# Rows scaled before they are transposed, half-slot waits split, and the router's gain moved into the rows

## The chip, the cores and the metric

The kernel runs on one core of a Trainium2 chip. The metric is device microseconds of one execution, lower is better; the time of a kernel is the median of its runs. The engines are TensorE (PE, its weight loads PEld), VectorE (DVE), ScalarE (ACT), GpSimd (POOL) and SyncE (SP), which here only issues the transfers of weights.

## The reference

Two blocks run on one sequence of 256 rows of width 1024, all in fp32. The first has two layers: attention and a gated convolution with a SwiGLU MLP (width 2816), then a spatial gating layer with a mixture of experts (eight SwiGLU experts of width 2816, two per row), each layer closed by a gated per-layer embedding. The second has two layers of four kinds of attention side by side and a squared-ReLU MLP of width 4096, modulated by columns that a vector `c` gives. Every part starts with an RMS norm:

```python
def rms_norm(x, g):
    xf = x.astype(jnp.float32)
    y = xf * lax.rsqrt(jnp.mean(xf * xf, axis=-1, keepdims=True) + RMS_EPS)
    return (y * g.astype(jnp.float32)).astype(x.dtype)
```

What matters here: x times one number per row, then times one number per column (in the second block also a column sum is added), then a product with weights.

## The kernel before, in words

**Weights.** They come as a stream of slots of 128x2048 fp32 (1 MB) into a ring of six in SBUF. SP waits until a slot has been split and refills it (L485 to L489). To multiply in fp32 precision, each half slot (128x1024) is split in two: ScalarE copies it rounded to fp32r as `w_hi` (L2001), VectorE subtracts to get `w_lo` (L1242). There are three pairs of such half buffers, four with the experts. A product is three matmuls, hi x hi, hi x lo and lo x hi (`product`, L515 to L519). `half_slot` (L510) makes TensorE wait until a half's `w_lo` is ready; ScalarE may write the next `w_hi` into a pair once the half in it is done. So a half buffer turns round in the order TensorE, ScalarE, VectorE, TensorE.

**Order.** Every engine's program is written out by hand, in one order; nothing is planned at run time. `split_to(m)` on ScalarE and VectorE puts the splits up to half m at that place of the program, and `reach(n)` says how far they can go when n halves are done.

**Norms.** There are eleven, numbered k = 0 to 10: 0 to 5 in the first block (4 is the router's), 6 to 9 in the second, 10 at the end. The rows lie in `resid`, 128 partitions x two row blocks t x 1024. `add_branch` (L1360) adds a layer's result, t = 0 first; ScalarE sums squares (`square_rows`), VectorE asks for the root (`ask_root`), POOL takes it (L2399). `scale` (L1299) then makes, for each t, a diagonal matrix `diag` of the 128 roots (L1310). `norm` calls it for t = 1 between two weight splits. On TensorE, `rowsT` (L529) multiplies each 128x128 block of the rows by `diag`, so that the block comes out in PSUM transposed and scaled in one (L537): four blocks of t = 0, then after a second wait four of t = 1, four of t = 0, four of t = 1. Ahead of it stand 18 dummy matmuls (`keep_warm`, L526) for k = 1, 6, 7, 9. From PSUM, ScalarE makes `x_hi` with the column gain (L2056), VectorE `x_lo` (L1351); in the second block both first modulate into `xT` (L1335 and L2048), then split (L2064 and L1349). For the router (k = 4) alone the rows themselves are scaled (L1303), transposed by the identity (L535) and multiplied by the gain into `xT` (L1329).

**The ends of a layer.** `row_product` goes through the halves of an output matrix; for a layer's output its last three go through `last_rows` (L601), and so do the last two of each MLP and of each embedding. It takes all its halves for row block 0 and then all for row block 1, so that block 0 is done early. It waits for all of its halves ahead of the first product (L603).

**Experts.** After the router, `select` (L1728) makes for each expert a 0/1 matrix `sel` from row to place in a chunk of 128, and `selg`, the same times the gate. TensorE's `gather` (L868) multiplies the scaled rows by `sel` into PSUM banks 6 and 7. `take` (L1738) on VectorE multiplies them by the norm's gain into `xT` (L1742), ScalarE's `take` (L2207) copies to `x_hi` (L2211), VectorE subtracts to `x_lo` (L1748). An expert has eleven steps j (`moe_step` on each engine): TensorE multiplies four halves up, transposes the previous step's hidden rows (L893), and multiplies two halves down. In step 6 of an expert VectorE selects for the next expert, in step 7 TensorE gathers, in step 8 both `take`. In step 1 VectorE splits the previous expert's result (`split_y`, L1764) behind the weight splits and ahead of the hidden rows' split (`moe_lo`, L1751); steps 2 and 3 scatter and merge. `selg` is read only by the second pass, a branch that runs when an expert has over 128 rows; these inputs don't take it.

## Time and profile before

| | |
|---|---|
| median of 3 runs | 2150.4 us (2150.29 to 2153.49) |
| the profiled execution | 2146.43 us, span 2144.7 us |
| granted TensorE clock, mean over the span | 0.966 |
| busy: PE, DVE, ACT, POOL | 1989.4, 1595.2, 1192.9, 27.9 us |

A line of a group gives the line of the kernel, the engine and operation, what is written from what, the count, and after the bar the busy time and the mean duration. In a timeline a line is one instruction or a run of equal ones: start, length, engine, line, operation, count, and in square brackets the idle time of the engine ahead of it and what ended it. A matmul's length is longer than the distance to the next, because they are pipelined; distances are read from starts. PEclk is the share of full speed (2.4 GHz) that was granted, 0.50 is 1.2 GHz.

### The profile page before, as it was taken

How to read it: one execution, taken by the hardware profiler on the slowest of the kernel's cores; microseconds unless marked ns; L12 is line 12 of the kernel's file. 1: busy time of each engine (PE TensorE's matmuls, PEld its weight loads, DVE VectorE, ACT ScalarE, POOL GpSimd, SP SyncE). 2: the span in 40 equal slices, each digit the busy share in tenths (PEclk: the TensorE clock that was granted, in tenths of full speed). 3: DMA queues.
4: the chain of work that ended last, by engine and by line, in shares of the span. 5: the costliest groups of instructions: out<-in, count | busy, mean ns of one | idle time of the engine just before them, and what ended most of it. 6: DMA issues, size and time to landing. Idle time of an engine off the chain costs nothing.

```text
span 2144.7 us, 28118 instructions
## 1 busy us (share of the span) xinstructions
PE 1989.4 (93%) x11190; PEld 1714.1 (80%) x11190; DVE 1595.2 (74%) x2014; ACT 1192.9 (56%) x1638; POOL 27.9 (1%) x32
## 2 busy tenths in 40 slices
PE   7879999976999999999999999898899999989998
PEld 7859998865878787878787777688789988868997
DVE  4657887455988989898989899568568984746555
ACT  4334334433877777777777778456444445634443
POOL 0000000000000000000000000000000000000000
PEclk9989999898999999999999999899999999989999
DMA  7416886432988888888888899433148973214551
GB/s 284 157 59 237 345 334 242 167 116 90 365 330 341 326 335 334 326 340 333 333 338 332 330 342 349 184 119 117 41 168 337 351 283 137 101 38 148 190 183 60
DMA packets 71263, 511.52 MB, mean 239 GB/s; under 512 B 8146, under 2 KB 8530, under 8 KB 9682
## 3 DMA queue, kind: packets, MB, share of 16 engines
q1 hardware_dynamic: 69536, 504.40, 62.4%
q10 hardware_dynamic: 1588, 5.24, 0.7%
q8 instruction: 91, 1.49, 0.3%
q14 instruction: 48, 0.39, 0.0%
HBM read 508.56 MB, written 1.05 MB: 238 GB/s over the span
## 4 chain that ended last, share of the span: by engine, by line
PE 79%; DVE 13%; ACT 5%; issue 2%; POOL 1%; DMA 0%; ACTq 0%; POOLq 0%; SPq 0%; DVEq 0%
PE ps L517 23%; PE ps L519 23%; PE ps L518 22%; DVE w_lo L1242 6%; ACT w_hi L2001 3%; PE ps L537 2%; PE ps L875 1%; PE ps L722 1%; PE ps L526 1%; PE ps L674 1%; PE ps L688 1%; PE ps L893 1%; PE ps L780 1%; ACT score L2109 1%; DVE arena L1228 1%
## 5 line engine op out<-in xcount | busy, mean ns | idle before, releaser
L1242 DVE TENSOR_TENSOR w_lo<-ring,w_hi 128x1024 fp32r<-128x1024 f32 x862 | 1043.2, 1222 | 373.3 <-ACT w_hi L2001 347.4
L2001 ACT ACTIVATE w_hi<-ring 128x1024 fp32r<-128x1024 f32 x862 | 909.9, 1060 | 704.9 <-PE ps L519 697.8
L517 PE MATMUL ps<-w_hi,x_hi 128*128 128x512 f32 (+1 forms) x1072 | 416.9, 391 | 29.1 <-DVE w_lo L1242 20.1
L519 PE MATMUL ps<-w_hi,x_lo 128*128 128x512 f32 (+1 forms) x1072 | 408.4, 383 | 0.0
L518 PE MATMUL ps<-w_lo,x_hi 128*128 128x512 f32 (+1 forms) x1072 | 407.9, 383 | 0.0
L517 PE MATMUL ps<-x_hi,w_hi 128*128 128x256 f32 x1248 | 357.9, 287 | 4.4 <-DVE x_lo L1351 3.8
L518 PE MATMUL ps<-x_lo,w_hi 128*128 128x256 f32 x1248 | 354.5, 284 | 0.0
L519 PE MATMUL ps<-x_hi,w_lo 128*128 128x256 f32 x1248 | 354.4, 284 | 0.0
L517 PE MATMUL ps<-w_hi,h_hi 128*128 128x512 f32 (+1 forms) x716 | 286.0, 399 | 23.0 <-DVE h_lo L1755 18.6
L518 PE MATMUL ps<-w_lo,h_hi 128*128 128x512 f32 (+1 forms) x716 | 279.4, 390 | 0.0
L519 PE MATMUL ps<-w_hi,h_lo 128*128 128x512 f32 (+1 forms) x716 | 279.2, 390 | 0.0
L517 PEld LDWEIGHTS ps<-w_hi,x_hi 128*128 128x128 f32 (+1 forms) x1072 | 197.4, 184 | 72.2 <-DVE w_lo L1242 24.3
L517 PEld LDWEIGHTS ps<-x_hi,w_hi 128*128 128x128 f32 x1248 | 241.0, 193 | 8.3 <-DVE w_lo L1242 4.0
L518 PEld LDWEIGHTS ps<-x_lo,w_hi 128*128 128x128 f32 x1248 | 240.9, 193 | 1.7 <-issue 0.2
L519 PEld LDWEIGHTS ps<-x_hi,w_lo 128*128 128x128 f32 x1248 | 240.6, 193 | 0.0
L519 PEld LDWEIGHTS ps<-w_hi,x_lo 128*128 128x128 f32 (+1 forms) x1072 | 197.2, 184 | 41.5
L518 PEld LDWEIGHTS ps<-w_lo,x_hi 128*128 128x128 f32 (+1 forms) x1072 | 197.7, 184 | 37.9
L517 PEld LDWEIGHTS ps<-w_hi,h_hi 128*128 128x128 f32 x716 | 134.7, 188 | 68.1 <-DVE h_lo L1755 37.2
L519 PEld LDWEIGHTS ps<-w_hi,h_lo 128*128 128x128 f32 x716 | 134.7, 188 | 29.0
L518 PEld LDWEIGHTS ps<-w_lo,h_hi 128*128 128x128 f32 x716 | 135.0, 189 | 24.4
L1228 DVE SCALAR_TENSOR_TENSOR arena<-ring,csilu,arena 128x1024 f32<-128x1024 f32 x88 | 108.9, 1278 | 0.0
L2109 ACT ACTIVATE score<-score,soft 128x128 f32<-128x128 f32 (+4 forms) x112 | 47.2, 423 | 35.5 <-DVE soft L1421 35.5
(266 smaller groups left out, 1490.6 us busy)
## 6 DMA issues: line engine op xcount, KB each, us to landing
ring<-in_stream SPq DMA_DIRECT2D x479, 1024.0 KB, 4.9
con<-in_consts ACTq DMA_DIRECT2D x1, 2048.0 KB, 21.6
resid<-in_x SPq DMA_DIRECT2D x1, 1024.0 KB, 6.3
arena<-in_ln_rows ACTq DMA_DIRECT2D x2, 512.0 KB, 4.5
arena<-in_fin_row ACTq DMA_DIRECT2D x2, 512.0 KB, 3.5
out<-rows SPq DMA_DIRECT2D x2, 512.0 KB, 2.6
arena<-in_w_s ACTq DMA_DIRECT2D x1, 512.0 KB, 5.7
con<-in_consts ACTq DMA_DIRECT2D x1, 237.0 KB, 4.1
```

Of the source, the lines that this page charges most:

```text
L517: pe.matmul(out_, lhs[0], rhs[0], start=start, stop=False)
L518: pe.matmul(out_, lhs[0], rhs[1], start=False, stop=False)
L519: return pe.matmul(out_, lhs[1], rhs[0], start=False, stop=stop)
L526: pe.matmul(ps[:, b, :], x_hi[:, 6, 0:P], x_lo[:, 4:6, :].rearrange("p a s -> p (a s)"), start=True, stop=True)
L537: return pe.matmul(at, src[:, t, c], diag[:, t, :], start=True, stop=True)
L674: last = pe.matmul(ps[:, b + u // 2, (u % 2) * S:(u % 2) * S + kw], q, k, start=True, stop=True)
L688: last = pe.transpose(ps[0:kp, 4 + n // 4, (n % 4) * P:(n % 4 + 1) * P], score[:, g % 2, u, kb * P:kb * P + kp], ident)
L722: last = pe.matmul(ps[:, mix_bank(layer, g), o * vw:(o + 1) * vw], probT[0:kp, g % 2, u * nkb + kb, :], v, start=kb == 0, stop=kb == nkb - 1)
L1228: ins = dve.scalar_tensor_tensor(out=acc[:, part, :], in0=src, scalar=c, in1=acc[:, part, :], op0=ALU.mult, op1=ALU.add)
L1242: dve.tensor_tensor(lo, ring[:, q % RING, a:a + HALF], hi.bitcast(F32), ALU.subtract)\
L2001: act.activation(half_buffer(m)[0], ring[:, q % RING, a:a + HALF], ACT.Copy).then_inc(hi_ready, 1)
L2109: ins = act.activation(sc, sc, ACT.Exp, bias=soft[:, g % 4, 0, u:u + 1], scale=96.0 ** -0.5 if kind == "mla" else 0.125, accum_out=soft[:, ...
```

## The change

It has four parts. `scale` writes scaled rows of 1024 in place of the diagonal, t = 0 in one operation and t = 1 in two halves (from `resid` to `rows`, in norm 6 from `rows` to `resid`), and `rowsT` transposes them by the identity in all norms, with a third wait before the last four blocks. `last_rows` waits for each half just ahead of its first product. The router's gain is read as a row spread over all partitions, into a buffer that the spatial layer's bias had; it goes into the rows with the scaling, so that what was a multiply after the transpose is a copy, and `take` reads PSUM directly on both engines. `selg` is left out of the first pass, and in step 1 `split_y` goes ahead of the last of four weight splits.

```diff
@@ build: names
+        moe_gain = ln_b
-        diag = ff[:, 2, 0:2 * P].rearrange("p (t s) -> p t s", t=QB)
@@ rowsT
                 def turn(t, f):
                     at = ps[:, 4 + f // 2, (f % 2) * S + t * P:(f % 2) * S + (t + 1) * P]
                     c = slice(f * P, (f + 1) * P)
-                    if k == 4:
-                        return pe.transpose(at, rows[:, t, c], ident)
-                    src = rows if k == 6 else resid
-                    return pe.matmul(at, src[:, t, c], diag[:, t, :], start=True, stop=True)
-
-                def scaled(t):
-                    if k == 4:
-                        pe.wait_ge(rows_scaled, t + 1)
-                    else:
-                        pe.wait_ge(diag_ready, 2 * NORM_AT[k] + t + 1)
+                    return pe.transpose(at, (resid if k == 6 else rows)[:, t, c], ident)
+
+                def scaled(n):
+                    pe.wait_ge(rows_scaled, 3 * k + n)
 
                 if k in (1, 6, 7, 9):
                     keep_warm(18, 2)
-                scaled(0)
+                scaled(1)
                 for f in range(4):
                     turn(0, f)
-                scaled(1)
+                scaled(2)
                 for f in range(KT):
                     if f == 4:
                         for late in range(4, KT):
                             turn(0, late)
+                        scaled(3)
                     last = turn(1, f)
@@ last_rows
-                w = [half_slot(m + n, 1) for n in range(len(lhs))]
+                w = []
                 for t in range(QB):
                     for n in range(len(lhs)):
+                        if t == 0:
+                            w.append(half_slot(m + n, 1))
                         row_part(w[n], t, lhs[n], b0, start and n == 0, n == len(lhs) - 1)
@@ VectorE: scale
-                if k == 4:
-                    dve.tensor_scalar(rows[:, t, :], resid[:, t, :], stat[:, t:t + 1], None, ALU.mult)\
-                        .then_inc(rows_scaled, 1)
-                elif k == 10:
+                if k == 10:
...
                 else:
                     r = stat[:, 2 * t + 1:2 * t + 2] if k == 6 else stat[:, t:t + 1]
-                    dve.tensor_scalar(diag[:, t, :], ident, r, None, ALU.mult).then_inc(diag_ready, 1)
+                    src, dst = (rows, resid) if k == 6 else (resid, rows)
+                    if k == 4:
+                        dve.wait_ge(moe_gain_in, 16)
+                        for c in (slice(0, BANK), slice(BANK, D)):
+                            ins = dve.scalar_tensor_tensor(out=rows[:, t, c], in0=resid[:, t, c], scalar=r,
+                                                           in1=moe_gain[:, c], op0=ALU.mult, op1=ALU.mult)
+                            if (t, c.start) != (0, 0):
+                                ins.then_inc(rows_scaled, 1)
+                        return
+                    for c in [slice(0, D)] if t == 0 else [slice(0, BANK), slice(BANK, D)]:
+                        dve.tensor_scalar(dst[:, t, c], src[:, t, c], r, None, ALU.mult).then_inc(rows_scaled, 1)
@@ VectorE: norm, k == 4
-                        src = ps[:, 4 + b, :].rearrange("p (f s) -> p f s", f=2)
-                        dve.tensor_tensor(xT[:, 2 * b:2 * b + 2, :], src, bc(gain[:, 2 * b:2 * b + 2], S), ALU.mult)\
+                        dve.tensor_copy(xT[:, 2 * b:2 * b + 2, :].rearrange("p f s -> p (f s)"), ps[:, 4 + b, :])\
                             .then_inc(gained, 1)
@@ VectorE: select
-                    dve.tensor_scalar(sel[:, t, :], rank, pl, None, ALU.is_equal)
-                    ins = dve.tensor_scalar(selg[:, t, :], rank, pl, gate[:, t, e], ALU.is_equal, ALU.mult)
+                    ins = dve.tensor_scalar(sel[:, t, :], rank, pl, None, ALU.is_equal)
+                    if w is second_pass:
+                        ins = dve.tensor_scalar(selg[:, t, :], rank, pl, gate[:, t, e], ALU.is_equal, ALU.mult)
@@ VectorE: take
-                for h in range(2):
-                    dve.wait_ge(w.gather_ready, counts[h])
-                    dve.tensor_tensor(xT[:, 4 * h:4 * h + 4, 0:P],
-                                      ps[:, 6 + h, :].rearrange("p (f c) -> p f c", f=4),
-                                      bc(gain(4)[:, 4 * h:4 * h + 4], P), ALU.mult).then_inc(w.gathered, 1)
                 for h in range(2):
                     dve.wait_ge(w.gathered_hi, counts[h])
                     f = slice(4 * h, 4 * h + 4)
-                    dve.tensor_tensor(x_lo[:, f, c0:c0 + P], xT[:, f, 0:P], x_hi[:, f, c0:c0 + P].bitcast(F32),
+                    dve.tensor_tensor(x_lo[:, f, c0:c0 + P], ps[:, 6 + h, :].rearrange("p (f c) -> p f c", f=4), x_hi[:, f, c0:c0 + P].bitcast(F32),
                                       ALU.subtract).then_inc(w.gathered_lo, 1)
@@ VectorE: moe_step
                 if s >= 1:
+                    if j == 1 and e >= 1:
+                        split_to(reach(2 * n + 1))
+                        split_y(e - 1)
                     split_to(reach(2 * (n + 1)))
-                    if j == 1 and e >= 1:
-                        split_y(e - 1)
                     moe_lo(s - 1)
@@ ScalarE: after the four Gelus of the spatial layer
+            act.wait_ge(vn_ready, 2)
+            act.dma_start(moe_gain, ln_rows[2].partition_broadcast(P)).then_inc(moe_gain_in, 16)
             keep_cat(4, 2)
@@ ScalarE: take
-                    act.wait_ge(w.gathered, counts[h])
+                    act.wait_ge(w.gather_ready, counts[h])
                     f = slice(4 * h, 4 * h + 4)
-                    act.activation(x_hi[:, f, c0:c0 + P], xT[:, f, 0:P], ACT.Copy).then_inc(w.gathered_hi, 1)
+                    act.activation(x_hi[:, f, c0:c0 + P], ps[:, 6 + h, :].rearrange("p (f c) -> p f c", f=4), ACT.Copy)\
+                        .then_inc(w.gathered_hi, 1)
```

The host packs the router's gain `lf[1]` as a third row of `ln_rows`.

## Rows read from the trace of the kernel before

**Rows 1.** The page, part 1: busy time of each engine.
```profile
PE 1989.4 (93%) x11190; PEld 1714.1 (80%) x11190; DVE 1595.2 (74%) x2014; ACT 1192.9 (56%) x1638; POOL 27.9 (1%) x32
```

**Rows 2.** Stretches: length, busy PE, PEld, DVE, ACT, POOL, PEclk, DMA share, GB/s.
```profile
500.00:527.00 27.00, 15.38 (x90) 14.36 (x90) 11.92 (x49) 4.15 (x10) 0.55 (x1) 0.68 0.00 0
...
527.00:1356.00 829.00, 798.17 (x3648) 644.59 (x3648) 739.68 (x792) 618.09 (x740) 0.00 (x0) 1.00 0.89 335
...
502.60:506.00 3.40, 2.73 (x12) 2.33 (x12) 2.34 (x4) 0.00 (x0) 0.00 (x0) 0.50 0.00 0
506.00:509.40 3.40, 3.11 (x28) 3.12 (x28) 0.23 (x1) 0.00 (x0) 0.00 (x0) 1.00 0.00 0
```

**Rows 3.** The waits of PE: releaser, us in total, times, longest.
```profile
PE ps L537 <- DVE ff L1310: 25.9, 9, 9.8
...
PE ps L517 <- DVE h_lo L1755: 18.6, 22, 1.3
```

**Rows 4.** Timeline of PE in `last_rows` ahead of norm 9.
```profile
1933.30 0.39 PE L519 MATMUL ps<-w_hi,x_lo 128*128 128x512 f32 x1
1936.25 0.76 PE L517 MATMUL ps<-w_hi,x_hi 128*128 128x512 f32 x1 [2.56 <-DVE w_lo L1242]
...
1937.23 0.63 PE L519 MATMUL ps<-w_hi,x_lo 128*128 128x512 f32 x1
```

**Rows 5.** The same in three other places.
```profile
151.85 0.47 PE L517 MATMUL ps<-w_hi,x_hi 128*128 128x512 f32 x1 [2.56 <-DVE w_lo L1242]
...
1560.89 0.76 PE L517 MATMUL ps<-w_hi,x_hi 128*128 128x512 f32 x1 [2.56 <-DVE w_lo L1242]
...
349.99 0.47 PE L517 MATMUL ps<-w_hi,h_hi 128*128 128x512 f32 x1 [0.67 <-DVE w_lo L1242]
```

**Rows 6.** Timeline of DVE, the first expert, behind the gather and in step 8.
```profile
594.58 1.23 DVE L1242 TENSOR_TENSOR w_lo<-ring,w_hi 128x1024 fp32r<-128x1024 f32 x1 [3.42 <-ACT w_hi L2001]
...
605.87 1.28 DVE L1742 TENSOR_TENSOR xT<-ps,con 128x512 f32<-128x512 f32 x2
607.25 1.29 DVE L1748 TENSOR_TENSOR x_lo<-xT,x_hi 128x512 fp32r<-128x512 f32 x2
608.80 4.63 DVE L1242 TENSOR_TENSOR w_lo<-ring,w_hi 128x1024 fp32r<-128x1024 f32 x4 [0.26 <-ACT w_hi L2001]
```

**Rows 7.** Timeline of ACT in the same step 8.
```profile
604.27 0.37 ACT L2235 ACTIVATE arena<-ps 128x256 f32<-128x256 f32 x1
606.59 1.23 ACT L2211 ACTIVATE x_hi<-xT 128x512 fp32r<-128x512 f32 x2 [1.95 <-DVE xT L1742]
```

**Rows 8.** Timeline of PE in the same step and the next.
```profile
608.60 0.38 PE L893 MATMUL ps<-con,arena 128*128 128x128 f32 x2
610.08 0.50 PE L517 MATMUL ps<-w_hi,x_hi 128*128 128x512 f32 x1 [1.10 <-DVE w_lo L1242]
...
613.82 0.50 PE L517 MATMUL ps<-w_hi,h_hi 128*128 128x512 f32 x1 [0.70 <-DVE h_lo L1755]
```

**Rows 9.** Timeline of PE: twelve blocks behind the second wait, norms 4, 7, 8.
```profile
502.54 2.79 PE L535 MATMUL ps<-con,rows 128*128 128x128 f32 x12 [1.64 <-DVE rows L1303]
...
1576.40 2.95 PE L537 MATMUL ps<-ff,resid 128*128 128x128 f32 x24 [0.58 <-DVE ff L1310]
...
1767.05 5.46 PE L537 MATMUL ps<-ff,resid 128*128 128x128 f32 x24 [1.78 <-DVE ff L1310]
```

**Rows 10.** DVE's lines by source: durations in ns (least, median, most), first and last start.
```profile
L1310 DVE TENSOR_SCALAR ff<-con,stat x18: 277/284/289, 9.4 to 1951.4; 128x128 f32<-128x128 f32 x18
...
L1303 DVE TENSOR_SCALAR rows<-resid,stat x2: 746/750/753, 499.4 to 501.7; 128x1024 f32<-128x1024 f32 x2
...
L1735 DVE TENSOR_SCALAR arena<-con,place,gate x16: 337/341/345, 518.8 to 1207.7; 128x128 f32<-128x128 f32 x16
```

**Rows 11.** Timeline of DVE in norm 7, behind the weight split.
```profile
1577.39 0.99 DVE L1335 TENSOR_SCALAR xT<-ps,modg,ada 128x256 f32<-128x256 f32 x2
```

More of the change, by code:

```diff
@@ L340, in build @@
         ln_in = sem("ln_in")
+        moe_gain_in = sem("moe_gain_in")
         fin_in = sem("fin_in")
@@ L412, in __init__ @@
                 self.gather_ready = sem(name + "gather_ready")
-                self.gathered = sem(name + "gathered")
                 self.gathered_hi = sem(name + "gathered_hi")
@@ L2606, in lay_out @@
         "lam": np.ascontiguousarray(np.asarray(i["a_lambda"])[0].reshape(-1)),
-        "ln_rows": np.stack([np.asarray(i["c_ln_g"])[0], np.asarray(i["c_ln_b"])[0]]),
+        "ln_rows": np.stack([np.asarray(i["c_ln_g"])[0], np.asarray(i["c_ln_b"])[0], lf[1]]),
         "w_s": np.ascontiguousarray(np.asarray(i["c_w_s"])[0].transpose(2, 0, 1)),
```

1 line of the change is left out of this document (removed).

## The prediction, made before the changed kernel was run

> **What bounds the kernel now.** The page's busy line comes first [rows 1]: TensorE works in 93% of the span, VectorE in 74%. So the time is TensorE's work, its clock, and the holes in it; a microsecond is won where TensorE waits or works less. The stage table shows where the holes are small in share but many: the experts' 829 us have TensorE busy for 798.2 of them, at full clock, with VectorE busy for 739.7 [rows 2]. The waits of TensorE name the releasers: 25.9 us in nine waits for the diagonal (one for each norm but the router's), and 18.6 us for `h_lo` L1755, nearly all with the experts [rows 3]. The timeline then shows single places: the last halves of a branch [rows 4, 5], the gather for the next expert [rows 6 to 8], the transposes of the rows [rows 9] and VectorE's part of them [rows 10, 11].
>
> **Part 1: waits one by one in last_rows.** Now the call waits for all its halves, then multiplies. In the branch before the last norm the previous product would have been followed at 1933.53 (start 1933.30 plus a pitch of 0.23), but the next starts at 1936.25, when the third half's `w_lo` is in [rows 4]. Halves one and two were split before, or that wait would name them in turn. Each is six matmuls in the first row block, 6 x 0.227 = 1.36 us, so with single waits TensorE reaches the third half at 1933.53 + 2.72 = 1936.25, just as it is ready. The hole closes: 2.72 us, and 0.08 for the slower first pitch behind a hole. Here and at 1560.89 the granted clock also fell to 1.2 GHz behind the hole (two matmuls from 1936.25 to 1937.23 take 0.98, against 0.46 at 2.4 GHz [rows 4]); eight such matmuls at 0.43 for 0.23, an estimate, are 1.6 us more. In the other two branches the matmul behind the hole has its full-clock length, 0.47 against 0.76 us [rows 5], and nothing more is won. Four branches: 2 x 2.8 + 2 x 4.35 = 14.3. Two calls with two halves (the first MLP's end, at 349.99, and one like it) wait 0.67 for the second half [rows 5]: about 0.9 each, 1.8. The third such call and the two of the gated embedding show no hole: 0. What is behind the waits on TensorE's queue is the same; ScalarE and VectorE wait for the second row block as before, and all move up. Sum **-16.1**; bounds 13 (the clock falls anyway, and 0.4 us stays at each third half) and 18.
>
> **Part 2: the gain leaves the gather.** In step 8 of seven experts VectorE multiplies two halves (1.28 us), ScalarE, idle for 1.95, copies them, and VectorE subtracts (1.29); its split of weights starts at 608.80 only [rows 6, 7]. TensorE has done its pair of transposes at 608.60 and should go on some 0.14 later (an estimate, as no hole-free pair is among the rows), but goes on at 610.08, and at 613.82, after 12 matmuls and another hole, where it would without one be at about 612.95 [rows 8]. The loss is 1.34 + 0.86 + 2 x 0.07 = 2.34 us. After: ScalarE copies from PSUM right behind the activation at 604.27, so 604.64 to 605.87; the subtraction can start where the multiply did, 605.87, and ends at 607.16. Four splits, 4.63, end at about 611.75 (their `w_hi` come in time, since ScalarE is 1.85 earlier), and `h_lo` at 612.05 to 612.15. TensorE wants it at 608.74 + 12 matmuls = 611.5: a loss of 0.6 to 0.7 stays. Won: 1.66 x 7 = **-11.6**. From below 0.8 each (a source in PSUM slows ScalarE, or the backlog is paid in the next step), from above 2.3: 5.6 to 16. The `selg` operations (341 ns, two per expert [rows 10]) go away in step 6; the gather hides them, as VectorE idles for 3.42 us behind it [rows 6]: 0. The exchange of split_y with the fourth split changes no total before `h_lo`, as three splits still come first: 0, bounds 0.7 either way in seven places. Ahead of the first expert nothing hides this chain: one 0.34 that no longer delays the gather plus its neighbour's issue, and one multiply: **-1.2**.
>
> **Part 3: the router's norm.** Two products of whole rows (750 ns [rows 10]) become two pairs of halves with the gain row, about 0.7 each by the 0.64 to 0.69 of a 512-wide operation with two inputs [rows 6]. The first pair's excess lies beside ScalarE's squares; in the second TensorE starts on the first half, at the same time. The four gain multiplies become copies of as many elements. Taken 0, bounds -0.4 and +0.5. The added transfer (ScalarE's queue, 0.5 MB spread over partitions) waits for VectorE's last use of that buffer; ScalarE's next work then is the concatenation, for which it waits anyway: 0. It lands tens of microseconds ahead of its use. SP's and POOL's queues get nothing new; POOL only sees its roots asked for 0.47 later in two norms where VectorE's whole-row product is directly ahead (the first and the sixth); the sixth pays it, and it is in the sum below.
>
> **Part 4: transposes for the diagonal, nine norms.** A 128x128 product with the diagonal is two matmul records, a transpose one: x24 is twelve blocks [rows 9]. At full clock twelve take 2.95 us, at 1.2 GHz 5.46; twelve transposes took 2.79 at 1.2 GHz, so half. TensorE saves 1.5 or 2.7 us behind the second wait. Against it VectorE: 283 ns become 0.75 us for row block 0 and two halves of some 0.48 for block 1 (between 283 and 750 ns by elements), of which the first delays the transposes by 0.2 and both delay the weight split behind them by 0.6. How it comes out depends on what follows:
> - Plain norms at full clock (the second and third): TensorE ended after the first `x_lo`, so it gains, until VectorE paces it: -0.3 and -0.5.
> - Modulated norms at full clock (before each MLP): the modulation starts at 1577.39 with no idle time ahead of it, right behind the weight split [rows 11]. VectorE is the bound, the 0.6 is lost: +0.6 each, +1.2.
> - Five norms at 1.2 GHz (first, fourth, sixth, and the first of each block): 2.7 less 0.2 to 0.6, and less what the products now do at the low clock, as they begin before it rises (the 5.46 us of [rows 9] all ran low): 1.0 to 2.0 each, taken 1.4: -7.0.
> Sum **-6.6**, bounds -11 and +3.
>
> What row and rule say of the clock differs here. The router's twelve transposes ran from 502.54 at 1.2 GHz and were nearly all that TensorE did up to 505.3; from 506.0 the granted clock was 2.4 GHz [rows 2, 9]. So transposes do bring it up, and I count them as work. The Trainium skill, TensorE: Matmul & The Clock Gate, Part 4: PE-mode transpose, says that a transpose does not count as busy for the clock; by it the time would be the first rival's, 2124, and this row disagrees.
>
> **Sum.** 16.1 + 11.6 + 1.2 + 6.6 = 35.5 us. The profiled execution took 2146.4 (span 2144.7 and 1.7 around it), so 2110.9 in its measure. The median of the three runs is 2150.4, 4.0 above it; I take the difference off the median: **2115 us**.
>
> **Rivals.**
> 1. Transposes leave the clock low. Then it rises only some 5 us (the 5.46 of [rows 9]) after the first product, not after the first transpose: in five norms about 3.4 us more at 0.43 in place of 0.23, 1.6 us each, and a little in two of the warm ones: +9, **2124**. Against it stands the router's row. 0.12.
> 2. The gather's gain is eaten: VectorE is busy for 89% of the experts' stage, and the hole moves into the next steps. Only part of Part 2 stays, 0 to 3: **2125**. For it: 18.6 us of waits for `h_lo`, which are a backlog's. Against it: before the gather VectorE idles over 3 us per expert. 0.11.
> 3. VectorE paces every norm: each of nine loses 0.6 and gains nothing: +5.4 for -6.6, **2127**. The two modulated ones show it; the others start `x_lo` behind waits for TensorE or ScalarE. 0.07.
> 4. Slower: the clock in the norms. TensorE has half the work there, and its holes could put each of ten norms and the products behind it at 1.2 GHz for as long as the router's stage was, 27 x (1 - 0.68) / 0.5 = 17 us [rows 2]. Each such microsecond loses (0.43 - 0.23) / 0.43 = 0.47: 10 x 17 x 0.47 = 80, less the 28.9 of the other parts: **2201**. It decides from 28.9 / 4.7 = 6 us per norm. The full clock kept through four norms speaks against it. 0.02.
> 5. Nothing changes, since the halves are late one by one as well, and scaling eats the rest: **2150**. The third half's wait speaks against it. 0.03.
>
> **The numbers.** Forecast 0.62, its own range 2108 to 2122; more than that won 0.03. A measurement of this kernel tells about 0.2% (4.3 us) from no change. Faster: 0.62 + 0.03 + 0.12 + 0.11 + 0.07 = 0.95, same 0.03, slower 0.02. The range reaches over the second and most of the third rival: 2106 to 2128.
>
> **What would show it.** Part 1: no hole over 0.3 us before the third half of a branch, and no 1.2 GHz stretch behind it. Part 2: ScalarE's L2209 copies right behind the silu, the 1.10 hole gone, one of about 0.6 before `h_lo`. Part 4: x12 records in 1.3 us (full clock) or 2.6; first product 1.0 to 2.3 us earlier at low clock; the modulation 0.6 later before the MLPs. I am wrong if holes of a microsecond stand in steps 9 and 10 of the experts, or if the clock stays low long into the products.

## The result, and the profile after

The changed kernel takes **2113.5 us**, the median of 4 runs (2110.5 to 2114.8), where the kernel before, in runs beside it, takes 2151.9 (2150.3 to 2153.7): ratio 0.9819, 95% interval 0.9802 to 0.9836. The forecast was 2115.0 with 2106 to 2128 around it. The profiled execution took 2114.8 us, with a span of 2113.0 where before it was 2144.7.

The page's busy line, to be read against [rows 1]:

```profile
PE 1970.7 (93%) x11046; PEld 1695.0 (80%) x11046; DVE 1592.0 (75%) x1993; ACT 1192.9 (56%) x1638; POOL 26.9 (1%) x32
```

TensorE issues 144 matmuls fewer (nine norms, 16 blocks each) and is busy for 18.7 us less; VectorE is busy for only 3.2 less. So of the 31.7 us between the two profiled spans 18.7 are work and clock, and some 13 are holes.

The waits of PE (releaser, us in total, times, longest), against [rows 3]:

```profile
PE ps L533 <- DVE rows L1313: 27.0, 9, 10.2
PE ps L516 <- DVE h_lo L1753: 15.8, 22, 1.4
...
PE ps L533 <- DVE resid L1313: 5.1, 2, 2.6
```

The wait for VectorE in the norms did not shrink: 25.9 us for the diagonal are 32.1 for the scaled rows, as scaling takes longer than a diagonal. What shrank there is the work behind it. The wait for `h_lo` fell by 2.8.

The stretches of the router and of the experts (length, busy PE, PEld, DVE, ACT, POOL, PEclk, DMA share, GB/s), against [rows 2]:

```profile
487.00:514.00 27.00, 17.28 (x90) 16.26 (x90) 10.72 (x46) 3.40 (x9) 0.55 (x1) 0.62 0.00 1
514.00:1331.00 817.00, 795.58 (x3648) 643.95 (x3648) 728.10 (x764) 618.84 (x741) 0.00 (x0) 1.00 0.90 340
```

The experts' 3648 matmuls need 817 us where they needed 829, at full clock in both. The router's 27 us have a mean clock of 0.62 where it was 0.68.

**The third half of a branch**, ahead of norm 9, on PE's timeline (start, duration), against [rows 4]:

```profile
1905.64 0.39 PE L518 MATMUL ps<-w_hi,x_lo 128*128 128x512 f32 x1
1905.86 0.39 PE L516 MATMUL ps<-w_hi,x_hi 128*128 128x512 f32 x1
1906.09 0.39 PE L517 MATMUL ps<-w_lo,x_hi 128*128 128x512 f32 x1
```

The matmul at 1905.86 is the one that stood at 1936.25 behind 2.56 us of waiting. It follows at a pitch of 0.22, and behind it the clock is full. The four holes of this kind and the two of 0.67 us are gone.

**The gather in step 8** of the first expert: DVE, then ACT, then PE, against [rows 6 to 8]:

```profile
593.38 1.28 DVE L1746 TENSOR_TENSOR x_lo<-ps,x_hi 128x512 fp32r<-128x512 f32 x2
594.58 4.62 DVE L1238 TENSOR_TENSOR w_lo<-ring,w_hi 128x1024 fp32r<-128x1024 f32 x4
599.12 0.42 DVE L1753 TENSOR_TENSOR h_lo<-ps,h_hi 128x256 fp32r<-128x256 f32 x1
```
```profile
591.78 0.36 ACT L2237 ACTIVATE arena<-ps 128x256 f32<-128x256 f32 x1
592.04 1.08 ACT L2212 ACTIVATE x_hi<-ps 128x512 fp32r<-128x512 f32 x2
```
```profile
596.13 0.38 PE L889 MATMUL ps<-con,arena 128*128 128x128 f32 x2
...
599.59 0.50 PE L516 MATMUL ps<-w_hi,h_hi 128*128 128x512 f32 x1 [0.33 <-DVE h_lo L1753]
```

ScalarE copies right behind its silu, VectorE subtracts once and splits on. The hole of 1.10 us is gone, and the one ahead of `h_lo` is 0.33.

**Two norms.** PE in norm 7 (the eighth, at full clock), against [rows 9]; DVE in the same norm, against [rows 11]; PE in norm 0:

```profile
1546.20 0.60 PE L533 MATMUL ps<-con,rows 128*128 128x128 f32 x4
1548.04 1.53 PE L533 MATMUL ps<-con,rows 128*128 128x128 f32 x12 [1.24 <-DVE rows L1313]
1551.02 0.36 PE L516 MATMUL ps<-x_hi,w_hi 128*128 128x256 f32 x1 [1.45 <-DVE x_lo L1351]
```
```profile
1547.49 0.88 DVE L1313 TENSOR_SCALAR rows<-resid,stat 128x512 f32<-128x512 f32 x2 [0.45 <-POOL stat L2401]
1548.29 1.22 DVE L1238 TENSOR_TENSOR w_lo<-ring,w_hi 128x1024 fp32r<-128x1024 f32 x1
1549.42 0.99 DVE L1337 TENSOR_SCALAR xT<-ps,modg,ada 128x256 f32<-128x256 f32 x2
```
```profile
13.39 2.82 PE L533 MATMUL ps<-con,rows 128*128 128x128 f32 x12 [2.06 <-DVE rows L1313]
20.13 0.55 PE L516 MATMUL ps<-x_hi,w_hi 128*128 128x256 f32 x1 [3.92 <-DVE x_lo L1353]
```

Twelve transposes take 1.53 us at full clock and 2.82 at 1.2 GHz, for 2.95 and 5.46 before. In norm 7 TensorE then stands for 1.45 us, since VectorE's chain of scaling, weight split and modulation is what ends last; in norm 0 the first product is 2.0 us nearer.

**Where the 31.7 us went.** The n-th main product (L517 before, L516 after) is the same work in both kernels, so the starts of one product in the two traces give a running balance. In the stretches named "other work" the change touches nothing:

| stretch | change, us |
|---|---|
| norm 0, with the ten products behind it | -2.65 |
| first attention and its projection (other work) | -1.3 |
| last halves of the four branches | -2.7, -2.7, -4.1, -4.2 |
| second halves of the two final downs | -0.7, -0.7 |
| norms 1, 2, 3 | -0.5, -0.65, -3.7 |
| spatial layer (other work) | +1.8 |
| router with the first gather | +0.6 |
| seven gathers and the experts' steps | -12.15 |
| norms 5, 6, 7, 8, 9 | -0.95, -1.6, +0.5, -2.1, +0.5 |
| attention of the two blocks (other work) | +2.7, +3.0 |

Part 1 has 15.1 us, the experts 12.15, the norms 11.15, and 6 to 7 us are given back where nothing was changed: there the stretches at 1.2 GHz lie elsewhere and are longer. The experiments ask which of these are the parts' own.

### The profile page after: what moved, and what is told of

Same layout as the page of the kernel before. It is cut to its first block, busy times and chain, and to the rows that moved or that the text cites. A ratio compares the mean times of both kernels' runs of the same rounds, so it can differ in the third digit from the quotient of the medians.

```text
span 2113.0 us, 27808 instructions
## 1 busy us (share of the span) xinstructions
PE 1970.7 (93%) x11046; PEld 1695.0 (80%) x11046; DVE 1592.0 (75%) x1993; ACT 1192.9 (56%) x1638; POOL 26.9 (1%) x32
## 4 chain that ended last, share of the span: by engine, by line
PE 79%; DVE 13%; ACT 5%; issue 2%; POOL 1%; DMA 0%; POOLq 0%; ACTq 0%; SPq 0%; DVEq 0%
PE ps L516 24%; PE ps L518 23%; PE ps L517 23%; DVE w_lo L1238 6%; ACT w_hi L2000 2%; PE ps L871 2%; PE ps L718 1%; PE ps L670 1%; PE ps L525 1%; PE ps L684 1%; PE ps L889 1%; ACT score L2108 1%; POOL stat L2401 1%; PE ps L776 1%; PE ps L533 1%
## 5 line engine op out<-in xcount | busy, mean ns | idle before, releaser
L516 PE MATMUL ps<-w_hi,x_hi 128*128 128x512 f32 (+1 forms) x1072 | 416.3, 391 | 11.6 <-DVE x_lo L1507 5.7
L517 PE MATMUL ps<-w_lo,x_hi 128*128 128x512 f32 (+1 forms) x1072 | 407.8, 383 | 0.0
L516 PE MATMUL ps<-x_hi,w_hi 128*128 128x256 f32 x1248 | 357.9, 287 | 8.6 <-DVE x_lo L1353 4.4
L517 PE MATMUL ps<-x_lo,w_hi 128*128 128x256 f32 x1248 | 354.2, 284 | 0.0
L516 PE MATMUL ps<-w_hi,h_hi 128*128 128x512 f32 (+1 forms) x716 | 285.4, 399 | 18.7 <-DVE h_lo L1753 15.8
L517 PE MATMUL ps<-w_lo,h_hi 128*128 128x512 f32 (+1 forms) x716 | 279.2, 390 | 0.0
L516 PEld LDWEIGHTS ps<-x_hi,w_hi 128*128 128x128 f32 x1248 | 240.4, 193 | 14.6 <-DVE w_lo L1238 5.0
L517 PEld LDWEIGHTS ps<-x_lo,w_hi 128*128 128x128 f32 x1248 | 240.6, 193 | 1.7 <-issue 0.2
L516 PEld LDWEIGHTS ps<-w_hi,x_hi 128*128 128x128 f32 (+1 forms) x1072 | 197.7, 184 | 52.4 <-DVE x_lo L1507 6.4
L517 PEld LDWEIGHTS ps<-w_lo,x_hi 128*128 128x128 f32 (+1 forms) x1072 | 197.8, 184 | 37.9
L516 PEld LDWEIGHTS ps<-w_hi,h_hi 128*128 128x128 f32 x716 | 134.5, 188 | 62.7 <-DVE h_lo L1753 34.4
L517 PEld LDWEIGHTS ps<-w_lo,h_hi 128*128 128x128 f32 x716 | 134.7, 188 | 24.4
L2108 ACT ACTIVATE score<-score,soft 128x128 f32<-128x128 f32 (+4 forms) x112 | 47.2, 423 | 38.5 <-DVE soft L1423 38.4
```

Of the source, the lines that this page charges most:

```text
L516: pe.matmul(out_, lhs[0], rhs[0], start=start, stop=False)
L517: pe.matmul(out_, lhs[0], rhs[1], start=False, stop=False)
L2108: ins = act.activation(sc, sc, ACT.Exp, bias=soft[:, g % 4, 0, u:u + 1], scale=96.0 ** -0.5 if kind == "mla" else 0.125, accum_out=soft[:, ...
```

## The experiments

Each ratio is against the kernel before, run beside it on the same chip, with its 95% interval.

**1. Part 1 alone.** The kernel before with

```diff
-                w = [half_slot(m + n, 1) for n in range(len(lhs))]
+                w = []
...
+                        if t == 0:
+                            w.append(half_slot(m + n, 1))
```

> The kernel before with the single waits of last_rows and nothing else. Theory of the forecast (each part gives its own term): 16.1 us less, ratio 0.9925 (bounds 13 to 18 us: 0.9940 to 0.9916); no hole before the third half of the four branches, none of 0.67 us at the two final downs. Rival (the term was oversized, since two changed profiles laid side by side show these places 15.0 us nearer and the low clock of other places drifts): 12 to 15 us, ratio 0.9944 to 0.9930. Rival (the waits only move the hole to the next half): under 5 us, ratio over 0.9977.

Measured: 2133.2 us for 2149.7, 16.5 less, ratio 0.992 (0.9906 to 0.9934). The waits of PE for `w_lo`, which this edit is about, and for `h_lo`, which it leaves alone:

```profile
PE ps L517 <- DVE h_lo L1757: 18.6, 22, 1.3
...
PE ps L517 <- DVE w_lo L1244: 9.9, 8, 2.5
```

The forecast's term stands. The eight waits that are left for `w_lo` are the seven of the gather, at 1.1 us or less, and one of 2.5 in the first attention.

**2. Parts 2 and 3 alone** (the gain row, the copies, `take` and the missing `selg` as in the change), with the diagonal, the joint waits and the old place of `split_y`. Of its edits, cut short, the one in ScalarE's `take`:

```diff
-                    act.wait_ge(w.gathered, counts[h])
-                    act.activation(x_hi[:, f, c0:c0 + P], xT[:, f, 0:P], ACT.Copy)...
+                    act.wait_ge(w.gather_ready, counts[h])
+                    act.activation(x_hi[:, f, c0:c0 + P], ps[:, 6 + h, :]..., ACT.Copy)...
```

> The kernel before with the router's gain in the scaled rows and the gather split straight out of PSUM, diagonal and joint waits as before, order of split_y as before. Theory of the forecast: 11.6 + 1.2 us less, ratio 0.9940; per expert the hole before the step 9 products (1.10 us) gone and the one before h_lo at 0.3 to 0.7 us. Rival (the gain in the experts is real, but the router's stage gives back: a longer stretch at 1.2 GHz): about 11 us, 0.9949. Rival (the experts' gain of the changed kernel came from the new order of split_y): under 6 us, over 0.9972.

Measured: 2136.3 for 2149.7, 13.4 less, ratio 0.9938 (0.9925 to 0.9952). The experts' stage is the cleanest ruler of this case, as it runs at full clock throughout: from its first product (527.26 before) to the first product behind the seventh gather's `h_lo` (1235.59 before) it is 708.33 us in the kernel before and 696.31 here, 12.0 less, or 1.72 per gather. The waits of PE for `h_lo` are those of the changed kernel:

```profile
PE ps L519 <- DVE h_lo L1758: 15.8, 22, 1.4
```

The router's stage, from the last product ahead of it to the first expert's first, was 31.6 us long here and 29.9 before, but 33.0 with Part 1 alone, which does not touch it. In both runs the clock was low for longer in that stage than in the profile of before. Where it was low at the same places, Parts 2 and 3 take 1.0 us off: 31.56 here and 32.56 in the run of experiment 9, which lacks them. So the rival that has this part give back there falls.

**3. The diagonal back** in the changed kernel's nine norms (`scale` writes `diag` again, and `rowsT` has two waits again):

```diff
-                    return pe.transpose(at, (resid if k == 6 else rows)[:, t, c], ident)
+                    return pe.matmul(at, src[:, t, c], diag[:, t, :], start=True, stop=True)
```

> The changed kernel with the diagonal again in the nine norms, the rest as changed. Theory of the forecast: Part 4 alone is worth 6.6 us, so 2120.1 us where the changed kernel has 2113.5, ratio to the kernel before 0.9852. Rival (from the two profiles side by side: fourth norm 3.7 us, first 2.6, not 1.4): 9 us, so 2122.5, ratio 0.9863. Rival (the norms gain nothing, the stretches at 1.2 GHz only change places): 2113 to 2115, ratio 0.9820 to 0.9828.

Measured: 2117.3 us (2117.0 to 2121.4), ratio 0.9857 (0.9842 to 0.9872). Against the changed kernel (0.9819 here, 0.9825 in experiment 5) that is 0.0035 or 7.5 us by the ratios, and 2 to 4 us by the medians. Norm 0, on PE's timeline, shows the whole of it as before:

```profile
13.22 4.88 PE L538 MATMUL ps<-ff,resid 128*128 128x128 f32 x24 [1.36 <-DVE ff L1320]
22.00 0.56 PE L518 MATMUL ps<-x_hi,w_hi 128*128 128x256 f32 x1 [3.90 <-DVE x_lo L1360]
```

The wait for the diagonal is 0.7 us shorter than the one for rows (1.36 for 2.06), the work behind it 2.06 longer (4.88 for 2.82), and the first product 1.87 later.

**4. The two edits taken at nothing**, undone in the changed kernel: `split_y` behind the fourth split again, `selg` in every expert again.

```diff
+                    split_to(reach(2 * (n + 1)))
                     if j == 1 and e >= 1:
-                        split_to(reach(2 * n + 1))
                         split_y(e - 1)
-                    split_to(reach(2 * (n + 1)))
...
-                    if w is second_pass:
+                    if True:
```

> The changed kernel with split_y behind the fourth split again, and with selg computed in the first pass again. Theory of the forecast: both are worth nothing, 2113 to 2114 us, ratio 0.982. Rival: the new order is what keeps the step 1 hole at 1.34 us, and without it up to 0.7 us are lost in seven places: 2118, ratio 0.9843. Rival: selg delays the split behind it in step 6, 0.34 x 2 x 7 = 4.8 us, the same 2118, but the hole would show in step 6 or 7 and not in step 1.

Measured: 2115.6 us, ratio 0.9843 (0.983 to 0.9857). By the ratio alone this could be a few microseconds. By the ruler (the 708.33 us stretch of experiment 2) it is nothing: 696.37 us, where the changed kernel has 696.18 and 696.05. Ahead of the first expert, outside that stretch, `selg` shows: the router's stage takes 29.23 us where experiment 10's kernel, with the clock low at the same places, takes 28.97. The waits for `h_lo` are 15.8 us in 22 again.

**5. The changed kernel once more.** No edit.

> The changed kernel again, beside the three others of this call. Theory: ratio 0.982 as before, and its profile differs from the first one only in where the stretches at 1.2 GHz begin and how long they are (by 3.4 or 6.8 us here and there, 0.47 of that in time). Rival: the profile is the same to 0.1 us, and the differences between the kernels' low-clock stretches are the kernels' own.

Measured: 2115.3 us (2106.4 to 2115.5), ratio 0.9825 (0.9799 to 0.985). The view of spans and mean granted clocks gives, for the first profile and for this one:

```profile
core 0: 2113.0 us, clock 0.967
```
```profile
core 0: 2113.7 us, clock 0.964
```

A mean of 0.967 means 0.033 x 2113 / 0.5 = 139 us at 1.2 GHz, one of 0.964 means 152: 13 us apart in the same program. The balance between the two profiles is 0.9 us nearer at the router's end, 2.0 further away ahead of the second attention, 2.0 nearer behind it, 0.7 further away at the end. So the first theory holds: stretches at 1.2 GHz move between executions of one program and shift work that no edit touches, here by 4 us over the second attention. The 6 to 7 us of "other work" in the table above are of that kind and size, though no run separates them, and a single profile can't price a part below some 2 us unless it lies at full clock.

**6. `h_lo` ahead of the fourth split in step 1** of experts 2 to 8, in the changed kernel:

```diff
                         split_to(reach(2 * n + 1))
                         split_y(e - 1)
+                        moe_lo(s - 1)
                     split_to(reach(2 * (n + 1)))
-                    moe_lo(s - 1)
+                    if j != 1 or e == 0:
+                        moe_lo(s - 1)
```

> The changed kernel, in step 1 of experts 2 to 8 h_lo ahead of the fourth weight split. Theory (VectorE's order is what leaves 1.34 us seven times): the fourth split's 1.22 leave the way of h_lo, the hole shrinks to 0.1 to 0.3, about 7 x 1.1 = 7.7 us less, 2106, ratio 0.9785. Rival (backlog: the split is then late for the next products): the hole moves to the next weight wait in step 2, 0 to 3 us less, 2111 to 2113. Rival (h_lo then waits for ScalarE's h_hi, which stands behind its own splits): 2113.

Measured: 2099.1 us, ratio 0.977 (0.975 to 0.9789). DVE in the second expert's step 1, changed kernel and this one, and between them PE's product behind it in the changed kernel:

```profile
623.90 1.28 DVE L1767 TENSOR_TENSOR y_lo<-ps,y_hi 128x512 fp32r<-128x512 f32 x2
625.10 1.22 DVE L1238 TENSOR_TENSOR w_lo<-ring,w_hi 128x1024 fp32r<-128x1024 f32 x1
626.24 0.42 DVE L1753 TENSOR_TENSOR h_lo<-ps,h_hi 128x256 fp32r<-128x256 f32 x1
```
```profile
626.71 0.50 PE L516 MATMUL ps<-w_hi,h_hi 128*128 128x512 f32 x1 [1.34 <-DVE h_lo L1753]
```
```profile
622.95 1.28 DVE L1767 TENSOR_TENSOR y_lo<-ps,y_hi 128x512 fp32r<-128x512 f32 x2
624.15 0.41 DVE L1753 TENSOR_TENSOR h_lo<-ps,h_hi 128x256 fp32r<-128x256 f32 x1
624.48 1.22 DVE L1238 TENSOR_TENSOR w_lo<-ring,w_hi 128x1024 fp32r<-128x1024 f32 x1
```

TensorE waited 1.34 us for `h_lo` there; here the hole is 0.20, and no later one grew. The ruler reads 689.45, for 696.18: 6.7 us in the six of the seven places that it spans, and to the last product of the last expert it is 7.9 in seven. The backlog rival falls. The medians are 16.2 us apart (2115.3 beside it), twice what was expected, and the edit explains only half of that. The means are 11.8 apart, and the five executions of this kernel had a mean clock of 0.969, for 0.966 in the changed kernel's five; by the 44 executions of the kernel before on record, which last 1.4 us longer for each 0.001 of mean clock less, that is some 4 to 5 us. Whether the edit or chance brought the clock is open.

**7. Without the warming products**, and **8. with transposes in their place.** In the changed kernel:

```diff
-                if k in (1, 6, 7, 9):
-                    keep_warm(18, 2)
```
```diff
-                    keep_warm(18, 2)
+                    for i in range(36):
+                        pe.transpose(ps[:, 2, (i % 4) * P:(i % 4 + 1) * P], x_lo[:, 4 + i % 2, 0:P].bitcast(F32), ident)
```

> The changed kernel without the 18 warming products ahead of four norms (second, seventh, eighth, tenth), which leaves out only work whose result nobody reads. Theory (TensorE idles there, and idling brings the granted clock to 1.2 GHz): a low stretch appears at the second, eighth and tenth norm, the transposes and the first products run at half speed, 1 to 3 us each, 3 to 9 us more in all, ratio 0.9835 to 0.986. Rival (the products of the branches just before keep the clock up through the wait anyway): nothing changes, and then the next run tells nothing.

> The changed kernel with the 18 warming products (about 4.1 us) replaced by 36 transposes of 128x128 (36 x 0.108 = 3.9 us). Theory of the forecast (transposes count as work for the clock): full clock at the second, eighth and tenth norm as with products, time within 1 us of the changed kernel, ratio 0.982. Rival (the rule of the Trainium skill, TensorE: Matmul & The Clock Gate, Part 4: PE-mode transpose, that a transpose does not count as busy for the clock): the same low stretches as in the run without warming, ratio 0.9835 to 0.986.

Measured: 2112.7 us without, ratio 0.9835 (0.9816 to 0.9853); 2112.8 with transposes, 0.9836 (0.9817 to 0.9856). Norm 7 without warming, a stretch (columns as above) and PE's timeline:

```profile
1545.50:1552.30 6.80, 5.46 (x24) 5.08 (x25) 6.21 (x14) 4.19 (x11) 0.60 (x1) 0.50 0.43 154
```
```profile
1544.24 0.66 PE L533 MATMUL ps<-con,rows 128*128 128x128 f32 x4 [3.31 <-DVE rows L1311]
1546.68 2.82 PE L533 MATMUL ps<-con,rows 128*128 128x128 f32 x12 [1.78 <-DVE rows L1311]
1549.67 0.55 PE L516 MATMUL ps<-x_hi,w_hi 128*128 128x256 f32 x1 [0.16 <-DVE x_lo L1349]
```

And with 36 transposes in place of the products:

```profile
1541.00:1551.30 10.30, 8.92 (x66) 7.98 (x64) 9.38 (x15) 6.02 (x10) 2.03 (x2) 1.00 0.26 93
```
```profile
1543.97 4.10 PE L540 MATMUL ps<-con,x_lo 128*128 128x128 f32 x36
1547.91 0.60 PE L533 MATMUL ps<-con,rows 128*128 128x128 f32 x4
1549.88 1.53 PE L533 MATMUL ps<-con,rows 128*128 128x128 f32 x12 [1.38 <-DVE rows L1314]
```

Idle for 3.31 us, TensorE falls to 1.2 GHz (0.50 from 1545.5 on). Kept busy with transposes alone through that wait, it stays at 1.00 until the products have begun, in norms 1 and 9 too. (Behind norm 7 the clock falls later, at 1555.0; with the warming products it does the same in the changed kernel's second profile, at 1551.3.) So the clock is held through the wait by transposes as by products. That is the forecast's reading of the router's row [rows 2, 9], now shown by a run made for it. The rule of the Trainium skill, TensorE: Matmul & The Clock Gate, Part 4: PE-mode transpose, that they do not count as busy for the clock, does not hold for these fp32 transposes.

What I had not expected is that the low clock in norms 7 and 9 costs next to nothing, and 0.5 us in norm 1. From a product ahead of the norm to one behind it (the measure of the table in experiment 9) norm 7 takes 19.22 us without warming and 19.17 with, norm 9 19.13 and 19.15, norm 1 15.83 and 15.37. The warming products end up to 0.7 us after the rows are scaled (VectorE ends the first block at 1545.54, the transposes begin at 1546.20), and with them the 1.45 us hole ahead of the first product stands where the slower transposes would have been.

**9. Part 4 alone.** The kernel before with

```diff
-                    dve.tensor_scalar(diag[:, t, :], ident, r, None, ALU.mult).then_inc(diag_ready, 1)
+                    src, dst = (rows, resid) if k == 6 else (resid, rows)
+                    for c in [slice(0, D)] if t == 0 else [slice(0, BANK), slice(BANK, D)]:
+                        dve.tensor_scalar(dst[:, t, c], src[:, t, c], r, None, ALU.mult).then_inc(rows_scaled, 1)
```

> The kernel before with scaled rows and transposes in the nine norms and nothing else. Theory of the forecast: 6.6 us less, ratio 0.9969. Rival (what the run without Part 1 and the run without Part 2 leave of the whole change, 0.0142 of 0.0180): 8 us, ratio 0.9962. Rival (what the changed kernel with the diagonal back showed in its medians): 3 to 4 us, ratio 0.9984. In its profile each place is 1.8 to 2.3 us nearer behind the first norm, 0.5 behind the second, 0.5 behind the third, and 0.6 further away behind the eighth and tenth.

Measured: 2148.7 us for 2151.2 in 12 runs (2145.6 to 2157.0), ratio 0.9993 (0.9978 to 1.0009). That is at most 4.7 us of gain, below the forecast's 6.6. The profiled execution, one of the three longest, has this view of spans and clocks, and these stretches around norm 7 here and, in the second fence, in the kernel before:

```profile
core 0: 2155.1 us, clock 0.956
```
```profile
1580.00:1594.00 14.00, 10.97 (x62) 9.52 (x61) 10.52 (x22) 7.25 (x18) 1.47 (x1) 0.88 0.21 77
```
```profile
1574.00:1588.00 14.00, 13.16 (x102) 12.20 (x101) 9.29 (x18) 7.24 (x17) 1.47 (x1) 1.00 0.28 99
```

TensorE has 2.2 us less to do in the 14, and the clock falls in them. Over the span 0.956 is 190 us at 1.2 GHz, against 146 before. At 0.47 us for each that is up to 44 x 0.47 = 21 us given back by this execution. But this profile is an extreme one, and most of its 44 us lie in the attentions and the router's stage and not in the norms. Over all executions the mean clock is 0.9604 (12) for 0.9632 (17 of the kernel before), some 12 us more at 1.2 GHz. By the 1.4 us per 0.001 of experiment 6 that costs some 4 us, and executions of equal mean clock (0.961 to 0.964) are 2 to 5 us shorter with Part 4 than without. So Part 4 gains in the norms here too, and the clock takes most of it back. The nine norms themselves, between two products that are the same work in all kernels, one ahead of the norm and one behind it (us):

| norm | before | Part 4 alone | changed, diagonal back | changed |
|---|---|---|---|---|
| 0 | 28.45 | 25.02 | 28.11 | 25.80 |
| 1 | 15.91 | 17.05 | 15.86 | 15.37 |
| 2 | 13.52 | 13.00 | 13.40 | 12.87 |
| 3 | 46.03 | 44.14 | 44.31 | 42.41 |
| 5 | 39.40 | 40.02 | 41.17 | 38.37 |
| 6 | 41.08 | 39.58 | 40.34 | 39.56 |
| 7 | 18.56 | 20.36 | 18.58 | 19.17 |
| 8 | 21.43 | 19.96 | 20.65 | 19.83 |
| 9 | 18.53 | 20.13 | 18.57 | 19.15 |

Between the two last columns Part 4 gains 2.3 + 0.5 + 0.5 + 1.9 + 2.8 + 0.8 + 0.8 and loses 0.6 twice: 8.4 us. (Norm 5's 2.8 is the least certain: the changed kernel's second profile has 39.97 there.) Between the two first it gains 8.8 in norms 0, 2, 3, 6 and 8, and loses 1.8 and 1.6 in norms 7 and 9, 1.1 in norm 1 and 0.6 in norm 5. That leaves 3.6, before what happens elsewhere. In norms 1, 7 and 9 the clock falls in the norm or just ahead of it. In norm 1 that is not Part 4's doing: Parts 2 and 3 alone, which keep the diagonal, have 17.50 there, behind the same stretch at 1.2 GHz. Behind norm 7 the clock never fell in the four profiles with the diagonal (before, and experiments 1, 2 and 3), and it fell in four of nine with transposes and warming: this one, the changed kernel's second (19.97 us) and those of experiments 6 and 8 (20.16 and 20.17). Behind norm 9 it fell only here.

**10. The weight split of the modulated norms behind the last `x_lo`:**

```diff
-                if next_half is not None:
+                if next_half is not None and shift is None:
                     split_to(next_half + 1)
...
+                    if f == KT - 1 and shift is not None and next_half is not None:
+                        split_to(next_half + 1)
```

> The changed kernel, in the four modulated norms with the weight split that stands between scaling and modulation behind the last x_lo. Theory (in these norms VectorE is the bound, as the forecast had it): at the eighth and tenth norm the hole of 1.45 us before the first product closes, x_lo ends 1.2 earlier, and the late split costs 0.7 of it: 0.5 each there, 0 to 0.5 each at the other two, 1 to 2 us less in all, 2112, ratio 0.9815. Rival (the late split and the following ones make the second half-slot late by all of 1.2): nothing or slower, 2113.5 to 2115. Rival (TensorE's transposes are the bound): the first product does not move.

Measured: 2112.4 us, ratio 0.9815 (0.9795 to 0.9835): the same as the changed kernel, within 1 or 2 us. Norm 7 on PE's timeline:

```profile
1547.94 0.60 PE L533 MATMUL ps<-con,rows 128*128 128x128 f32 x4
...
1552.00 0.35 PE L516 MATMUL ps<-x_hi,w_hi 128*128 128x256 f32 x1 [0.69 <-DVE x_lo L1351]
```

From the first transpose to the first product it is 4.06 us, for 4.82: VectorE was the bound there. Seventeen products behind, 0.88 us are kept in norms 7 and 9 (18.29 and 18.28 in the table's measure), and 0.35 are lost in norms 6 and 8 (39.90 and 20.19), where the transposes run at 1.2 GHz and the late split is the one that is missed.

**11. `h_lo` ahead of the last split in every step:**

```diff
+                    split_to(reach(2 * n + 1))
                     if j == 1 and e >= 1:
-                        split_to(reach(2 * n + 1))
                         split_y(e - 1)
-                    split_to(reach(2 * (n + 1)))
                     moe_lo(s - 1)
+                    split_to(reach(2 * (n + 1)))
```

> The changed kernel with h_lo ahead of the last weight split in every step of the first pass. Theory (VectorE's order sets every h_lo hole): besides the 1.14 us in step 1 also the 0.33 (step 9), 0.44 (step 4) and 0.93 (last step) go, 7 x 0.77 + 0.8 = 6 us beyond the run with step 1 alone, 2093, ratio 0.9742. Rival (VectorE is busy nearly throughout and the splits become late instead, the hole moves to w_lo): 0 to 2 us beyond it, 2097 to 2099. Rival (h_lo now waits for ScalarE's h_hi, and the split behind it with it, in steps that had no hole): slower than step 1 alone, over 2101.

Measured: 2091.9 us, ratio 0.972 (0.9697 to 0.9743). The stretch of the experts, 3648 matmuls:

```profile
514.00:1308.00 794.00, 786.34 (x3648) 647.87 (x3648) 718.78 (x764) 618.23 (x740) 0.00 (x0) 1.00 0.91 350
```

It is 23 us shorter than in the changed kernel; 8 were expected from experiment 6's seven places and 6 from these. From 624 us to 1297 the only holes over 0.1 us left on TensorE are six of 0.21, in step 1 of experts 3 to 8. What I had not counted is pitch: some 16 of the 22 are the holes and the slow first pitch behind them, and 5 are 51 pitches of about 0.33 us, in steps that showed no hole, which have become 0.23.

**12. Both orders together.** As 11, with the late split in norms 7 and 9 only, and in the last step

```diff
-            split_to(reach(2 * down_slot(STEPS - 1)))
+            split_to(reach(2 * down_slot(STEPS - 1) - 1))
             moe_lo(STEPS - 1)
+            split_to(reach(2 * down_slot(STEPS - 1)))
```

> The run with h_lo ahead of the last split in every step, with the last step's h_lo (0.93 us of waiting) ahead of its last split too, and with the late split of the modulated norms in the eighth and tenth alone, where it brought the first product 0.76 us nearer without a later wait. Theory: 0.8 + 2 x 0.76 = 2.3 us beyond the run without them, about 2089.5, ratio 0.971, and the holes of the experts from the first h_lo to the last stay closed. Rival (the stretches at 1.2 GHz decide more than these 2.3 us): within 3 us of the other run in either direction, 2089 to 2095. Rival (the closed holes of the last run were luck of one profile): holes of 0.3 to 1.3 us before h_lo again, 2099 and more.

Measured: **2087.7 us** (2083.6 to 2088.0), ratio 0.9699 (0.9684 to 0.9715), the fastest of all. The last step, on PE's, ACT's and DVE's timelines:

```profile
1299.30 0.44 PE L889 MATMUL ps<-con,arena 128*128 128x128 f32 x2
1299.77 0.39 ACT L2222 ACTIVATE h_hi<-ps 128x256 fp32r<-128x256 f32 x1 [1.85 <-PE ps L889]
1300.19 0.42 DVE L1755 TENSOR_TENSOR h_lo<-ps,h_hi 128x256 fp32r<-128x256 f32 x1 [0.95 <-ACT h_hi L2222]
```

The late split brings its 0.75 us in each of the two norms (the hole ahead of the first product is 0.70 for 1.45). The last step's hole of 0.93 us stays: VectorE idles for 0.95 us ahead of `h_lo`, because it waits for ScalarE's `h_hi`, which waits for TensorE's own transposes. No split stands in that chain, so the order of splits can't shorten it. The 4.2 us against experiment 11 are partly clock: 0.968 for 0.964 in the profiles, and 0.968 for 0.965 as means of five.

## Why the prediction was right, point by point

**Part 1, -16.1: right.** 16.5 us by itself, with an interval of 14.2 to 20.2. Every hole named is gone, and behind the third halves ahead of norms 7 and 9 the clock stays full; the two branches without that stretch gave 2.7 each (taken 2.8), the two with it 4.1 and 4.2 (taken 4.35), the final downs 0.7 each (taken 0.9).

**Part 2, -11.6: right, 12.0 measured.** The chain came out as worked out: the subtraction in VectorE's slot of the multiply, then four splits in 4.62 us, then `h_lo` 5.7 us behind the subtraction's start (599.12 less 593.38). I had TensorE want `h_lo` 0.25 us too early, so 0.33 us of hole stay where I said 0.6 to 0.7. The hole of the next steps didn't grow, so rival 2 fell. `selg` and the place of `split_y` are worth nothing, to 0.2 us in 696. The -1.2 ahead of the first expert shows where the clock was alike: from the last product ahead of the router to the first expert's, 29.90 us before and 28.95 in the second profile of the changed kernel, 1.0 less; in other profiles the low clock covers it. Some 0.3 of it is `selg` (experiment 4).

**Part 3, 0: right**, in as far as that same 1.0 us leaves 0.2 for it; no run has it apart from Part 2. That the gain row is read in time and ScalarE's queue loses nothing shows in the same place. ScalarE's copies out of PSUM, which I had feared slower, took 1.08 us for two (1.23 out of SBUF [rows 7]).

**Part 4, -6.6: right in its place, but its size hangs on what stands around it.** Norm by norm the terms hold: modulated norms at full clock lose 0.6 each (taken 0.6), plain ones gain 0.5 each (taken 0.3 and 0.5), the five at 1.2 GHz gain 8.6 together (taken 7.0; norms 0 and 3, with 2.3 and 1.9, were undersized at 1.4, norms 6 and 8, with 0.8, oversized). That is 8.4 of local gain from one pair of profiles, and 5.7 with the changed kernel's second profile, in which norm 5 gains 1.2 in place of 2.8 and the clock falls behind norm 7. At equal mean clock whole executions say 4 to 6: the changed kernel and the one with the diagonal back lie 3.6 us apart at 0.967 and 6.0 at 0.964, with one to three executions on a side. So the term is of the right size at equal clock. But alone, on the kernel before, Part 4 is worth 1.5 us with an interval that ends at 4.7. What I left out of the sum is a small form of my own rival 4: with less work in the norms TensorE can spend more time at the low clock. I had given it only as all or nothing, at 17 us per norm. The runs show it as 0.0028 of mean clock, some 4 us over the whole program (experiment 9). In the changed kernel no such price shows: the mean clock is 0.9666 in nine executions, and 0.9658 in four with the diagonal back. Why it is paid in one kernel and not in the other is not shown. That Part 1 has closed the holes ahead of norms 7 and 9 is one reading, but closed holes do not keep the clock up by themselves, as the changed kernel's second profile falls behind norm 7 all the same. The three parts by themselves have 16.5, 13.4 and 1.5, or 0.0149 by their ratios, and the whole has 0.0181, a difference that the intervals don't prove.

**The sum** of 35.5 us stands at 38.5 beside one set of runs of before and at 33.9 beside another (experiment 5). Parts 1 and 2 are right term by term. That the median came within 1.5 us of the forecast is also luck: the clock moved 6 to 7 us of other work in the first profile, and the changed kernel's executions reach from 2106.4 to 2115.5 us. Rival 1 is excluded by experiment 8, rival 3 by norms 1, 2 and 0, rival 5 by all.

## What to carry to other kernels

A stage in which the clock never moves is a ruler: measure an edit by the distance between two instructions that are the same work in both kernels, and it tells 0.2 us where whole runs tell 2 to 4. Where TensorE's holes are released by an engine that does several things in turn, look at what that engine does directly ahead of the releasing instruction: here one exchange in VectorE's order, a short operation that TensorE waits for ahead of a long one that it doesn't yet need, in every step of the experts, brought 22.6 us from the first of their products to the last, more than any part of the change. And work taken off TensorE can come back as low clock, in part or whole: look at the mean clock of all executions beside their times before a part is called worthless.

## What the runs showed of the hardware that was not expected

**The clock falls during one-column products.** Ahead of norm 3 TensorE sums columns in 64 products of one column each, without a hole. PE's timeline and two stretches in the changed kernel:

```profile
382.25 9.77 PE L776 MATMUL ps<-ones,arena 128*128 128x1 f32 x64
391.89 3.65 PE L533 MATMUL ps<-con,rows 128*128 128x128 f32 x16
```
```profile
380.00:386.00 6.00, 6.00 (x46) 5.61 (x44) 5.72 (x10) 4.59 (x9) 0.55 (x1) 1.00 0.14 59
386.50:391.80 5.30, 5.30 (x27) 5.30 (x27) 3.46 (x6) 0.69 (x3) 1.46 (x1) 0.50 0.00 0
```

TensorE is busy for all of 386.5 to 391.8, and the granted clock is 1.2 GHz from 386.5 on. The forecast had put norm 3 down as "at 1.2 GHz" and didn't ask why. TensorE did not idle before the fall (busy for 6.00 of 6.00 us from 380 on), and the transposes that follow start behind these products, not behind the scaling.

**Warming gives next to nothing here**, as experiment 7 shows: in norms 7 and 9, where TensorE waits for VectorE anyway, the low stretch costs under 0.1 us. No whole run tells the two kernels apart (2112.7 us without warming, 2113.5 and 2115.3 with).

**The low-clock stretches differ from execution to execution** of one program, by 13 us in two profiles of the changed kernel. In the router's stage they took the distance from the last product ahead of it to the first expert's to 28.95 to 33.04 us, in kernels with and without each part.
